# One layer of a hybrid decoder block on one core: how x is turned, how its third chunk of weights is split, and how dt is multiplied

## The reference, cut to what matters

```python
u = rms_norm(h, mix_norm_g)            # h is x, (1, 256, 1024)
proj = u @ w_in                        # (1024, 12320); xBC and dt among its columns
q, k, v, z, xbc, dt_raw, qm, gate_logits = jnp.split(proj, split_points, axis=-1)
dt = jax.nn.softplus(dt_raw + ssm_dt_bias)   # dt_raw: 32 columns, one for each SSD head
```

## Time and profile before

| | |
|---|---|
| median of three runs | 690.17 us |
| profiled execution, its own time | 690.53 us |
| its span, first to last instruction | 688.7 us |
| outside the span | 1.8 us |
| PE busy | 680.3 us, 99% |
| DVE busy | 492.8 us, 72% |
| ACT busy | 372.1 us, 54% |
| POOL busy | 9.9 us, 1% |
| mean granted TensorE clock | 0.998 of 2.4 GHz |

### The profile page before, as it was taken

How to read it: one execution, slowest core, us unless ns; L and a number is a source line. 1 busy time by engine, 2 the same in 40 slices (tenths; PEclk the granted TensorE clock), 3 DMA queues, 4 the chain that set the end, 5 groups by cost and what they waited for, 6 DMA issues and landing times.

```text
span 688.7 us, 11510 instructions
## 1 busy us (share of the span) xinstructions
PE 680.3 (99%) x4543; PEld 622.7 (90%) x4543; DVE 492.8 (72%) x614; ACT 372.1 (54%) x461; POOL 9.9 (1%) x22
## 2 busy tenths in 40 slices
PE   9999999999999999999999999999999999999996
PEld 7999999999999989899888888888898999999995
DVE  4886979696866766778655655456679777777796
ACT  6578777767555544564633333443456555555552
POOL 0000000000100000000000000000000000000001
PEclk9999999999999999999999999999999999999999
DMA  9775867569194445445566755575445555555521
GB/s 297 225 252 190 245 194 252 157 221 332 63 294 134 148 158 199 138 141 181 170 217 201 250 184 184 185 223 178 168 135 184 186 189 186 184 188 188 193 89 61
DMA packets 98825, 130.25 MB, mean 189 GB/s; under 512 B 5149, under 2 KB 73062, under 8 KB 98278
## 3 DMA queue, kind: packets, MB, share of 16 engines
q1 hardware_dynamic: 98022, 125.27, 56.3%
q10 hardware_dynamic: 768, 4.49, 1.7%
HBM read 128.65 MB, written 2.67 MB: 191 GB/s over the span
## 4 chain that ended last, share of the span: by engine, by line
PE 94%; DVE 2%; ACT 2%; DMA 1%; issue 0%; SPq 0%; POOL 0%; POOLq 0%; DVEq 0%; ACTq 0%
PE ps L358 29%; PE ps L359 29%; PE ps L360 29%; PE ps L663 1%; DVE w_lo L330 1%; DMA w_raw<-w_in 1%; ACT w_hi L326 1%; PE ps L648 1%; PE ps L664 1%; PE ps L700 1%; PE ps L683 1%; PE ps L413 0%; PE ps L691 0%; ACT h_sc L1208 0%; DVE h_nat L1710 0%
## 5 line engine op out<-in xcount | busy, mean ns | idle before, releaser
L330 DVE TENSOR_TENSOR w_lo<-w_raw,w_hi 128x2048 fp32r<-128x2048 f32 x108 | 247.0, 2288 | 91.0 <-ACT w_hi L326 91.0
L326 ACT ACTIVATE w_hi<-w_raw 128x2048 fp32r<-128x2048 f32 x108 | 206.3, 1911 | 97.8 <-PE ps L360 93.9
L358 PE MATMUL ps<-tok_hi,w_hi 128*128 128x256 f32 x864 | 247.1, 286 | 0.2 <-DVE tok_lo L1277 0.2
L359 PE MATMUL ps<-tok_lo,w_hi 128*128 128x256 f32 x864 | 244.4, 283 | 0.0
L360 PE MATMUL ps<-tok_hi,w_lo 128*128 128x256 f32 x864 | 244.4, 283 | 0.0
L358 PEld LDWEIGHTS ps<-tok_hi,w_hi 128*128 128x128 f32 x864 | 165.6, 192 | 2.3 <-issue 1.7
L359 PEld LDWEIGHTS ps<-tok_lo,w_hi 128*128 128x128 f32 x864 | 165.7, 192 | 0.4
L360 PEld LDWEIGHTS ps<-tok_hi,w_lo 128*128 128x128 f32 x864 | 165.6, 192 | 0.0
L358 PE MATMUL ps<-w_hi,tok_hi 128*128 128x512 f32 x128 | 50.2, 392 | 0.0
L359 PE MATMUL ps<-w_lo,tok_hi 128*128 128x512 f32 x128 | 49.9, 390 | 0.0
L360 PE MATMUL ps<-w_hi,tok_lo 128*128 128x512 f32 x128 | 49.8, 389 | 0.0
(11 more groups left out here) (267 smaller groups left out, 1010.5 us busy)
## 6 DMA issues: line engine op xcount, KB each, us to landing
w_raw<-w_in SPq DMA_DIRECT2D x94, 512.0 KB, 4.8
w_raw<-w_ffn_up SPq DMA_DIRECT2D x44, 512.0 KB, 4.0
w_raw<-w_ffn_down SPq DMA_DIRECT2D x22, 512.0 KB, 3.9
w_raw<-w_mem_kv SPq DMA_DIRECT2D x16, 512.0 KB, 4.4
w_raw<-w_br_ssm SPq DMA_DIRECT2D x16, 512.0 KB, 4.9
acs_b<-acs_d ACTq DMA_DIRECT2D x4, 1024.0 KB, 6.3
w_raw<-w_br_attn SPq DMA_DIRECT2D x8, 512.0 KB, 4.8
w_raw<-w_br_mem SPq DMA_DIRECT2D x8, 512.0 KB, 4.6
```

The lines of the kernel that those rows point to most:

```text
L326: act.activation(w_hi[:, s, :], w_raw[:, s, :], ACT.Copy).then_inc(hi_ready[s], 1)
L330: dve.tensor_tensor(w_lo[:, s, :], w_raw[:, s, :], w_hi[:, s, :].bitcast(F32), ALU.subtract).then_inc(lo_ready[s], 1)
L358: pe.matmul(o, a[0], b[0], start=start, stop=False, **kw)
L359: pe.matmul(o, a[0], b[1], start=False, stop=False, **kw)
```

## The change

x is no longer turned by a scaled identity: DVE multiplies x itself by the factor in place (tile 0 whole, tile 1 in two halves), and PE turns it with plain transposes, all but k = 7 of both tiles ahead of the first product. The third load is split in two halves on ACT and DVE, each behind its own DMA. The dt product no longer uses high and low parts: GpSimd adds `tok_hi` and `tok_lo` back to whole tokens `tok_full`, in two halves of k (four k of 256 tokens: 1024 elements in each partition), and PE does 8 fp32 matmuls with 32 stationary columns each; product k writes PSUM partitions 32(k mod 4) and on, so that four 32-column parts of the array are used in turn. `fold` now sums four parts in place of two.

```diff
-            dve.memset(wdt_both[:, :, 2 * SHEADS:P].bitcast(F32), 0.0).then_inc(wdt_rest, 1)
-            dve.wait_ge(const_in, 16)
-            for t in range(NT):
+            for t, cols in ((0, slice(0, D)), (1, halfcols(0)), (1, halfcols(1))):
                 dve.wait_ge(x_rstd, t + 1)
-                dve.tensor_scalar(diag[:, t, :], ident, stat[:, t:t + 1], None, ALU.mult).then_inc(diag_set, 1)
+                dve.tensor_scalar(x_nat[:, t, cols], x_nat[:, t, cols], stat[:, t:t + 1], None,
+                                  ALU.mult).then_inc(x_scaled, 1)
...
-            def turn_scaled(t, ks):
-
-                pe.wait_ge(diag_set, t + 1)
+            def turn_x(t, ks):
+
                 for k in ks:
-                    mm = pe.matmul(x_half(k)[:, t * P:(t + 1) * P], x_nat[:, t, k * P:(k + 1) * P], diag[:, t, :],
-                                   start=True, stop=True)
+                    pe.wait_ge(x_scaled, 1 + t + (k >= HK) * t)
+                    mm = pe.transpose(x_half(k)[:, t * P:(t + 1) * P], x_nat[:, t, k * P:(k + 1) * P], ident)
...
-            turn_scaled(0, range(5))
-            turn_scaled(1, range(4))
-            turn_scaled(0, range(5, 7))
+            turn_x(0, range(KT - 1))
+            turn_x(1, range(KT - 1))
             first_part(1, 0, range(1), (x_lo, 1))
-            for k in range(4, 7):
-                turn_scaled(1, range(k, k + 1))
-                first_part(1, 0, range(k - 3, k - 2), (x_lo, 1))
-            turn_scaled(0, range(7, KT))
-            turn_scaled(1, range(7, KT))
+            turn_x(0, range(KT - 1, KT))
+            turn_x(1, range(KT - 1, KT))
+            first_part(1, 0, range(1, HK), (x_lo, 1))
...
-            pe.wait_ge(wdt_rest, 1)
-            pe.wait_ge(wdt_lo_s, 1)
+            pe.wait_ge(dtw_in, 16)
+            pe.wait_ge(tok_summed, 2)
             for k in range(KT):
-                pe.matmul(ps[:, 4, 0:T], wdt_both[:, k, :], tok_hi[:, k, :], start=k == 0, stop=False)
-                mm = pe.matmul(ps[:, 4, 0:T], wdt_both[:, k, :], tok_lo[:, k, :], start=False, stop=k == KT - 1)
+                quarter = slice(k % 4 * SHEADS, (k % 4 + 1) * SHEADS)
+                mm = pe.matmul(ps[quarter, 4, 0:T], wdt_raw[:, k, :], tok_full[:, k, :], start=k < 4, stop=k >= KT - 4)
             mm.then_inc(dt_mm, 1)
...
+            pe.wait_ge(first_lo, 5)
             gemm_cols(pe, 0, 1, tok_hi, tok_lo, between=turn_dt)
...
-            act.wait_ge(dtw_in, 16)
-            act.activation(wdt_both[:, :, 0:SHEADS], wdt_raw[:], ACT.Copy).then_inc(wdt_hi_s, 1)
-            split_hi(act, 0, 1, first=True)
+            for n, done in ((0, first_hi), (1, hi_ready[1])):
+                ks = slice(n * CHUNK // 2, (n + 1) * CHUNK // 2)
+                act.wait_ge(third_in[n], 16)
+                act.activation(w_hi[:, 1, ks], w_raw[:, 1, ks], ACT.Copy).then_inc(done, 1)
...
-            dve.wait_ge(wdt_hi_s, 1)
-            dve.tensor_tensor(wdt_both[:, :, SHEADS:2 * SHEADS], wdt_raw[:], wdt_both[:, :, 0:SHEADS].bitcast(F32),
-                              ALU.subtract).then_inc(wdt_lo_s, 1)
-            dve.tensor_tensor(fold[0:2 * SHEADS, :], ident[0:2 * SHEADS, 0:SHEADS],
-                              ident[0:2 * SHEADS, SHEADS:2 * SHEADS], ALU.add).then_inc(fold_set, 1)
-            split_lo(dve, 0, 1)
+            dve.wait_ge(const_in, 16)
+            dve.tensor_reduce(fold[:], ident.rearrange("p (a h) -> p h a", h=SHEADS), AX, ALU.add).then_inc(fold_set, 1)
+            for n, ready, done in ((0, (first_hi, 4), first_lo), (1, (hi_ready[1], 1), lo_ready[1])):
+                ks = slice(n * CHUNK // 2, (n + 1) * CHUNK // 2)
+                dve.wait_ge(*ready)
+                dve.tensor_tensor(w_lo[:, 1, ks], w_raw[:, 1, ks], w_hi[:, 1, ks].bitcast(F32),
+                                  ALU.subtract).then_inc(done, 1)
...
+            for n in range(2):
+                ks = slice(n * HK, (n + 1) * HK)
+                pool.wait_ge(x_lo, (n + 1) * HK)
+                pool.tensor_tensor(tok_full[:, ks, :], tok_hi[:, ks, :].bitcast(F32), tok_lo[:, ks, :].bitcast(F32),
+                                   ALU.add).then_inc(tok_summed, 1)
             rstd(2, m_sumsq, m_var, m_rstd)
```

More of the change, by code:

```diff
@@ L164, in build @@
     junk_x = place("junk_x", R + 32.25, [NT, D + 1])
-    diag = place("diag", R + 42, [NT, P])
     cols_mix = place("cols_mix", R + 41, [KT])
     wdt_raw = place("wdt_raw", R + 8, [KT, SHEADS])
-    wdt_both = place("wdt_both", R + 12, [KT, P], F32R)
+    tok_full = place("tok_full", R + 0, [KT, T])
     fold = place("fold", R + 16, [SHEADS])
@@ L242, in build @@
     second_in = [sem("second_in0"), sem("second_in1")]
+    third_in = [sem("third_in0"), sem("third_in1")]
     first_hi, first_lo = sem("first_hi"), sem("first_lo")
@@ L246, in build @@
     zeros_set, small_set, squares_warm = sem("zeros_set"), sem("small_set"), sem("squares_warm")
-    wdt_rest, fold_set = sem("wdt_rest"), sem("fold_set")
+    tok_summed, fold_set = sem("tok_summed"), sem("fold_set")
     params_ready = sem("params_ready")
[L249 to L252, removed]
+    x_sumsq, x_rstd, x_scaled, x_turned, x_hi, x_lo = map(
+        sem, ("x_sumsq", "x_rstd", "x_scaled", "x_turned", "x_hi", "x_lo"))
+    dt_mm, dt_copied, dt_turned, dt_exp, dt_step, a_exp = map(
+        sem, ("dt_mm", "dt_copied", "dt_turned", "dt_exp", "dt_step", "a_exp"))
     acs_mm, acs_ready, acs_out, acs_in = map(sem, ("acs_mm", "acs_ready", "acs_out", "acs_in"))
@@ L322, in split_hi @@
     def split_hi(act, r, s, first=False):
-        act.wait_ge(loaded[s], 32 * (r + 1) if s else 32 * r)
+        act.wait_ge(loaded[s], 32 * (r + 1) if s > 1 else 32 * r)
         if not first:
@@ L464, in _ @@
             sp.dma_start(wdt_raw[:], wi[:, DTC:DTC + SHEADS].rearrange("(k p) n -> p k n", p=P)).then_inc(dtw_in, 16)
-            load(sp, 0, 1, wi, XC)
+            third = wi[:, XC:XC + CW].rearrange("(k p) n -> p k n", p=P)
+            slot = w_raw[:, 1, :].rearrange("p (k n) -> p k n", k=KT)
+            for n, ks in enumerate((slice(0, KT // 2), slice(KT // 2, KT))):
+                sp.dma_start(slot[:, ks, :], third[:, ks, :]).then_inc(third_in[n], 16)
             sp.dma_start(params[:], columns).then_inc(params_in, 16)
@@ L619, in turn_dt @@
                 for t in range(NT):
-                    mm = pe.matmul(ps[:, 6, t * SHEADS:(t + 1) * SHEADS], dt_raw[0:2 * SHEADS, t * P:(t + 1) * P],
-                                   fold[0:2 * SHEADS, :], start=True, stop=True)
+                    mm = pe.matmul(ps[:, 6, t * SHEADS:(t + 1) * SHEADS], dt_raw[:, t * P:(t + 1) * P],
+                                   fold[:], start=True, stop=True)
                 mm.then_inc(dt_turned, 1)
+            pe.wait_ge(first_lo, 5)
             gemm_cols(pe, 0, 1, tok_hi, tok_lo, between=turn_dt)
@@ L979, in _ @@
             act.wait_ge(dt_mm, 1)
-            act.activation(dt_raw[0:2 * SHEADS, :], ps[0:2 * SHEADS, 4, 0:T], ACT.Copy).then_inc(dt_copied, 1)
+            act.activation(dt_raw[:], ps[:, 4, 0:T], ACT.Copy).then_inc(dt_copied, 1)
             def load_acs(g):
```

## The result

The changed kernel took 692.55 us in the median against 690.57 for the kernel before in the same runs; the ratio is 1.0032 with a 95% interval of [1.0023, 1.0042], that is 1.6 to 2.9 us slower. The forecast was 693.0, by GpSimd and DVE shutting each other out: 2.8 us later than before, where 1.98 was measured. Its profiled execution spans 690.7 us (before 688.7). One execution of e8 (1358.02 us) and two of the kernel before run beside it (740.14 and 2388.66) were in a slow state, and no ratio uses them.

The account below looks back on a forecast made before the run. PE was taken to bound the kernel; its savings (0.88 + 0.7) vanish in waits for DVE, held up by GpSimd's sums, so 690.17 + 2.8 = 693.0 us. The 8-in-10 range was 688.8 to 694.5.

Parts of the forecast that it names:

- PE bound, a shift at the start is carried to the end: Whole kernel: PE, busy 99% of the span, sets the time; a start shift is neither absorbed nor grown later.
- x: 0.88 us less for PE, DVE's scaling hidden: Before PE's first product: fewer transposes save 0.88 us; DVE's idle 0.74 us covers scaling, `tok_lo` 0 starting 0.05 later.
- dt: 1.2 us with four parts at once: PE's dt product: 8 fp32 products, four at once 0.86, plus 0.12 going in and 0.20 coming back.
- The rival in which the 32-column parts do not run together: PE's dt product: parts run in turn, dt takes 3.44 + 0.3 us, 4.2 late, 694.4; chance 0.08.
- `turn_dt` costs what it did: Behind the dt product on PE: `turn_dt` and the copy were forecast to keep their earlier cost.
- Mutual blocking, and who comes next: GpSimd's sums and DVE's two-input subtractions exclude each other, waiting GpSimd goes next; main case, 2.8 us late, chance 0.47.
- A sum costs 2.33 us: GpSimd's sum of 1024 elements: 0.19 + 2.14 = 2.33 us, between bounds of 1.26 and 3.75.
- two reads in turn: Reason for the sum's 2.33 us: GpSimd reads its two operands one after another, through one stream.
- The size: slot 1 forecast 2.8 us late: Start of slot 1's `gemm_cols` on PE: forecast at 21.4 instead of 18.64, waiting for DVE's low part.
- The first rival's price: DVE is not stopped by GpSimd's sums: `turn_dt` 1.2 to 1.4 us earlier, 688.9 us; chance 0.28.
- No loss of clock in the gaps: PE's gaps of about 1.8, 1 and 1 us before slot 1 were counted as costing no clock.

Follow-up runs that it names:

- e8: Changed kernel with one sum on DVE behind the third load's halves instead of GpSimd's, dt product between slot 1's column halves; 690.64 us, ratio 1.000.
- e4: Kernel before with x scaled and transposed alone; 689.60 us, ratio 0.9986.
- e1: Changed kernel without GpSimd's two sums, dt product reading the high parts of the tokens alone; 688.62 us, ratio 0.9973.
- e6: Changed kernel with each GpSimd sum waiting for one more semaphore, a quarter of DVE's low-part subtraction; 691.46 us, ratio 1.0019.
- e2: Kernel before with the dt part alone (GpSimd's sums, 8 fp32 products in four parts), third load whole; 692.30 us, ratio 1.0029.
- e9: Changed kernel with GpSimd writing zeros (two memsets) in place of the sums, dt made of zeros; one execution, 689.60 us.
- e10: Changed kernel with GpSimd multiplying the high parts by 1.0 in place of the sums, low parts left out of dt; one execution, 690.43 us.
- e5: Kernel before, unchanged, profiled again to see when the third load lands; 690.23 us.
- e3: Kernel before with x scaled and transposed and the third load in halves, dt as before; 689.52 us, ratio 0.9988.
- e7: Changed kernel without GpSimd's sums, dt by 16 fp32 products on high then low tokens in four 32-column parts; 689.34 us, ratio 0.9989.

## Why the prediction came out right, step by step

- *PE bound, a shift at the start is carried to the end.* Right: slot 1 moved by 2.20 us, the span by 2.0, and PE's windows from 60 to 680 us are the same to 0.01 us. It holds for small shifts: in e8, with the dt chain 1.2 us late and PE's products early, PE idled 1.9 us at 80 to 90.
- *x: 0.88 us less for PE, DVE's scaling hidden.* Right. Scaling took 0.75 and 0.88 (two halves); e4 won 0.8 us. `tok_lo` began at 9.05, the 0.05 late that was worked out, but that it fits so well is luck: it began at 9.00 in e1 and at 8.80 in e6, as x came earlier or later.
- *dt: 1.2 us with four parts at once.* Right: 1.07 us for 16 records, and in e1, where slot 1 follows at once, 1.00 and 0.20 on the way back. The rival in which the 32-column parts do not run together fell. Not right was that `turn_dt` costs what it did: it and the product behind it are 0.31 shorter.
- *Mutual blocking, and who comes next.* Right, and shown by e1, e2, e6 and e9. At the first sum GpSimd, which had asked first, came through between two back-to-back subtractions, as in the earlier trace rows. By the SBUF — State Buffer page of the Trainium skill (Who interferes with whom) the holder keeps the other out to the end of its instruction; the runs agree that a GpSimd instruction that reads shuts out a two-input DVE instruction, and differ on the end: 0.84 us of DVE's time for a one-input GpSimd instruction recorded at 3.16 (2.6 net).
- *A sum costs 2.33 us.* The number was near (DVE was held 2.20 us by the first sum, and 2.10 by the second, from quarter (1,1)'s end at 16.28 to 20.73 - 2.35; e6's sums, which waited for nothing, are recorded at 2.42 and 2.37). Its reason was not: e10 shows that an operation with one input takes longer, so 'two reads in turn' does not make up GpSimd's time. What does stays open.
- *The size: slot 1 forecast 2.8 us late, measured 2.20; the time forecast 2.8 later, measured 1.98.* The term that was over-sized is DVE's chain, forecast to end at 21.35 and ended at 20.73: the two sums held DVE 0.36 less together; the rest is that DVE's quarter (1,1) was issued 0.08 before `tok_lo` had ended, where I took the gap of the kernel before, and smaller overlaps of that kind. The last 0.2 of the time is `turn_dt`.
- *That 692.55 lies so near to 693.0 is in part luck.* The forecast was added to 690.17, the median of three runs; in the seven that were run with the change it was 690.57. The shift itself was over-sized by 0.8 us, and the higher base hid 0.4 of that.
- *The first rival's price.* It was capped at 1.4 us by ACT's copy of dt behind slot 2's load, from a single profile's landing at 17.86. In e1 and e5 that load lands at 16.70, and e1, which is nearly that rival's schedule (without the sums), is 1.75 faster than before.
- *No loss of clock in the gaps.* Right for the profiled execution (1.00 from 12 to 25 us); not always, see below.

## What to carry to other kernels

Work given to an idle engine is not free if its reading shuts a busy one out: before moving an elementwise sum to GpSimd, list the DVE instructions with two SBUF inputs that follow its trigger, and add its reading to the first of them that it meets; put it beside DVE work that reads PSUM, or cut it small. A sum that only feeds TensorE may not be needed at all: 16 fp32 products in four 32-column parts cost 1.86 us. They beat the whole-token way, and are no slower than the 16 fp32r ones plus splits: e3 and e7 both span 687.6 us in their profiles, and their medians differ by 0.2 us, within their intervals. And one profile's DMA landing is one draw: profile the kernel before twice before calling two engines level. Of all that leaves nothing out of dt, e4, e3 and e7 are the fastest found (ratios 0.9986, 0.9988 and 0.9989), and the runs do not tell them apart.

## What the runs showed of the hardware that I had not expected

A fall of the clock after short gaps. e6's eleven executions fall into seven at 691.3 to 691.5 and four at 692.7 to 693.0; its profiled one is of the latter. Windows of e6:

```profile
18.00:19.00 1.00, 0.50 (x12) 0.01 (x3) 1.00 (x2) 1.00 (x2) 0.00 (x0) 1.00 1.09 374
...
20.00:21.00 1.00, 1.00 (x6) 1.00 (x6) 1.00 (x1) 1.00 (x3) 0.00 (x0) 0.50 0.50 63
...
22.00:23.00 1.00, 1.00 (x7) 1.00 (x6) 0.00 (x0) 0.00 (x0) 0.00 (x0) 0.50 1.08 380
```

The granted clock is at its lower level, 1.2 GHz, from about 19.6 to 23 us, and a product of 256 columns takes 0.21 us on the chain in place of 0.12. Before it PE had idled 0.58, 0.92 and 1.11 us between 14.2 and 19.6 us, with the 32-column products between the last two. Only the one execution was profiled; that the other three at 692.7 to 693.0 fell too is an inference from their time. The changed kernel idled longer (1.60, 0.64 and 1.10 us from 13.0 to 20.8) and kept its clock in the profile, so the gaps alone do not decide it. One of its seven executions took 693.87, 1.3 above the others, which may be the same, or a late x: in e9 x landed 1 us late, and single executions of the kernel before also lie 1.2 to 1.5 above its median.

A one-input GpSimd multiply by 1.0 of 1024 elements is slower than the two-input add (3.16 against 2.77, each with 0.5 us of waiting in it), and a memset of the same tile takes 0.96.
